# Weighted sum of expert rows: from full diagonal products to quarter products on two slots at a time

## What is computed

```
u = expert_down[idx]
act = jax.nn.gelu(jnp.einsum('thkd,td->thk', u, xb).astype(f32), approximate=False)
return jnp.einsum('thk,thkd->td', (g * act).astype(xb.dtype), expert_up[idx])
```

## Time and profile before

| | us |
|---|---|
| median of 3 runs | 4379.14 |
| lowest, highest | 4378.43, 4388.24 |
| span of the profiled execution | 4384.4 |
| PE busy | 3487.9 |
| DVE busy | 2354.8 |
| ACT busy | 1050.6 |
| POOL busy | 1348.0 |

### The profile page before, as it was taken

How to read it: one execution, slowest core, us unless ns; L and a number is a source line. 1 busy time by engine, 2 the same in 40 slices (tenths; PEclk the granted TensorE clock), 3 DMA queues, 4 the chain that set the end, 5 groups by cost and what they waited for, 6 DMA issues and landing times.

```text
span 4384.4 us, 39661 instructions
## 1 busy us (share of the span) xinstructions
PE 3487.9 (80%) x11633; PEld 1922.7 (44%) x11633; DVE 2354.8 (54%) x4730; ACT 1050.6 (24%) x3019; POOL 1348.0 (31%) x1232
## 2 busy tenths in 40 slices
PE   7699996469997687786787788778769778877876
PEld 1698774135555342352353344335325324324432
DVE  0651111746663767457546646646755755664574
ACT  1110112123341222222222222222222222222222
POOL 0020110400000343344444443434444444443442
PEclk9799997689998898898899889889889889988988
DMA  7232210642323899999999999999999999999996
GB/s 273 69 103 110 82 61 31 246 165 86 101 72 134 345 374 374 381 384 366 361 389 368 376 375 379 366 370 380 382 384 378 381 374 383 377 375 375 395 382 272
DMA packets 210634, 1269.30 MB, mean 290 GB/s; under 512 B 25875, under 2 KB 51099, under 8 KB 74060
## 3 DMA queue, kind: packets, MB, share of 16 engines
q0 software_dynamic: 159504, 1114.68, 64.3%
q1 hardware_dynamic: 50902, 152.03, 9.9%
HBM read 1218.26 MB, written 48.36 MB: 289 GB/s over the span
## 4 chain that ended last, share of the span: by engine, by line
DMA 26%; PE 25%; issue 8%; ACT 4%; POOL 3%; DVE 3%; POOLq 0%; ACTq 0%; DVEq 0%; SPq 0%
DMA e_buf<-in_experts,e_idx 26%; PE ps L1771 22%; PE ps L1502 3%; POOL e_buf L1738 3%; DVE e_buf L1840 2%; ACT e_wts L1812 2%; ACT e_diag L1816 1%; ACT e_acts L1810 1%; DMA e_buf<-in_experts,e_idxT 0%; DMA r_wq<-in_w_query 0%; POOLq L58 0%; DVE r_work L1590 0%; DVE r_row L1591 0%; DVE r_work L1587 0%; DVE r_pos L1550 0%
## 5 line engine op out<-in xcount | busy, mean ns | idle before, releaser
L1771 PE MATMUL ps<-e_buf,e_diag 128*128 128x512 f32 x4096 | 2026.0, 652 | 638.7 <-ACT e_diag L1816 635.2
L1840 DVE SCALAR_TENSOR_TENSOR e_buf<-e_buf,e_h 128x1024 f32<-128x1024 f32 x1024 | 1248.2, 1227 | 1091.6 <-DMA e_buf<-in_experts,e_idx 1075.2
L1738 POOL DMA_INDIRECT e_buf<-in_experts,e_idx x1024 | 1195.4, 1167 | 1605.1 <-PE ps L1771 1406.3
L1771 PEld LDWEIGHTS ps<-e_buf,e_diag 128*128 128x128 f32 x4096 | 836.0, 210 | 1758.4 <-issue 990.9
L1810 ACT ACTIVATE e_acts<-e_dots 128x4 f32<-128x4 f32 x256 | 52.6, 205 | 2085.0 <-DVE e_buf L1840 2076.4
L1816 ACT ACTIVATE e_diag<-ident,e_wts 128x128 f32<-128x128 f32 x1024 | 327.3, 390 | 27.8 <-ACT e_wts L1812 2.7
L1502 PEld LDWEIGHTS ps<-r_h2T,r_wq 128*128 128x128 f32 x2304 | 269.3, 193 | 34.0 <-issue 34.0
L1502 PE MATMUL ps<-r_h2T,r_wq 128*128 128x128 f32 x2304 | 269.9, 276 | 3.1 <-DMA r_wq<-in_w_query 3.1
L830 PE MATMUL ps<-xo_w_out,xo_catT 128*128 128x512 f32 x512 | 224.5, 592 | 1.7 <-DVE xo_x L863 1.7
L1812 ACT ACTIVATE e_wts<-e_acts,e_gate 128x1 f32<-128x1 f32 x1024 | 218.5, 284 | 9.2 <-ACT e_acts L1810 1.1
L74 PE MATMUL ps<-p_wth,hT_high 128*128 128x512 f32 (+1 forms) x432 | 170.6, 395 | 10.9 <-PEq L413 10.9
(11 more groups left out here) (338 smaller groups left out, 3007.2 us busy)
## 6 DMA issues: line engine op xcount, KB each, us to landing
w_mod_sb<-in_w_mod SPq DMA_DIRECT2D x12, 2048.0 KB, 8.4
e_buf<-in_experts,e_idx POOLq DMA_INDIRECT x1024, 9.1
p_wt<-in_w_rows SPq DMA_DIRECT2D x6, 2048.0 KB
proj_d<-p_ev POOLq DMA_DIRECT2D x48, 256.0 KB, 2.3
x_zgv<-proj_d SPq DMA_DIRECT2D x8, 1536.0 KB
p_w<-in_w_chan SPq DMA_DIRECT2D x20, 512.0 KB, 4.3
r_wq<-in_w_query SPq DMA_DIRECT2D x4, 2048.0 KB, 20.2
xbc_d<-p_res POOLq DMA_DIRECT2D x12, 516.0 KB, 3.0
```

Source lines behind the costliest of these rows:

```text
L1738: return pool.indirect_dma_start(out=buf[s][:], out_offset=None, in_=io["experts"], in_offset=bass.IndirectOffsetOnAxis(ap=numbers, axis=0 ...
L1771: last = nc.tensor.matmul(g.bank(cols), diag[:, k % RING, :], buf[k % RING][:, D + cols * 512:D + (cols + 1) * 512], start=(k == 0), stop= ...
L1840: V.scalar_tensor_tensor(out=down, in0=down, scalar=1.0, in1=row, op0=ALU.mult, op1=ALU.mult, accum_out=out).then_inc(sem, 1)
```

## The change

PE now takes two slots together, an even and an odd one. Each diagonal matrix is kept as its two 64x64 diagonal blocks side by side on the partitions (`diag` is 128 x 64 per slot, written from `eye2`, which has an identity in each half). A slot's sum over its upper 64 partitions and its lower 64 are separate products of 64x64 by 64x512. The even slot's products go to the partitions where their rows are, in banks 0 and 1; the odd slot's go to the other half of the partitions, in banks 2 and 3. So the four combinations of input half and output half, the quarters of the PE array, all occur. A pair has eight such products where two slots had four; PE waits for both diagonals and then releases both buffers with one increment of 2.

At the end of a tile the odd sums stand on the wrong halves. ACT copies banks 2 and 3 to `odd` (`keep_odd`), PE multiplies them with a swap matrix into banks 0 and 1 (`fold`), and DVE's `Finish.add` waits for that (`folded`) instead of `summed`. DVE builds `eye2` and `swap` once. The router's transposes move to banks 4 and 5 and wait for the scores before (`s_kept`).

PE, the first tile, before: a group of four slots, then a piece of routing. 128x512 is a product's output; each row is the program's, one per `matmul`.

```diff
--- before.py
+++ after.py
@@ -1479,8 +1479,10 @@
 
         g, nc = self.g, self.g.nc
         pe.wait_ge(self.h2_in, n * 16 + 16)
+        if not (isinstance(n, int) and n == 0):
+            pe.wait_ge(self.s_kept, n * 4)
         for k in range(KD):
-            last = nc.tensor.transpose(g.ps[:, 2 * 512 + k * P:2 * 512 + (k + 1) * P], self.h2[:, k * P:(k + 1) * P],
+            last = nc.tensor.transpose(g.ps[:, 4 * 512 + k * P:4 * 512 + (k + 1) * P], self.h2[:, k * P:(k + 1) * P],
                                        g.ident[:])
         last.then_inc(self.h2T_ps, 1)
         yield
@@ -1515,7 +1517,7 @@
 
         g, A = self.g, self.g.nc.scalar.activation
         act.wait_ge(self.h2T_ps, n + 1)
-        A(self.h2T[:].rearrange("p k r -> p (k r)"), g.ps[:, 2 * 512:4 * 512], ACT.Copy).then_inc(self.h2T_kept, 1)
+        A(self.h2T[:].rearrange("p k r -> p (k r)"), g.ps[:, 4 * 512:6 * 512], ACT.Copy).then_inc(self.h2T_kept, 1)
         yield
 
         def scores(b):
@@ -1682,7 +1684,9 @@
         buf = [sb(f"buf{s}", [P, 2 * D]) for s in range(RING)]
         idx, gate, h2 = sb("idx", [P, SLOTS], U32), sb("gate", [P, SLOTS]), sb("h2", [P, D])
         dots, acts, wts = sb("dots", [P, SLOTS]), sb("acts", [P, SLOTS]), sb("wts", [P, SLOTS])
-        diag = sb("diag", [P, RING, P])
+        diag = sb("diag", [P, RING, HALF])
+        eye2, swap, odd = sb("eye2", [P, HALF]), sb("swap", [P, P]), sb("odd", [P, D])
+        folds_ready, odd_kept, folded = sem("folds_ready"), sem("odd_kept"), sem("folded")
         h2_kept, idx_kept, generated = sem("h2_kept"), sem("idx_kept"), sem("generated")
         landed = [sem(f"landed{s}") for s in range(RING)]
         dotted, wch, weighed, summed = sem("dotted"), sem("wch"), sem("weighed"), sem("summed")
@@ -1761,26 +1765,42 @@
         def _(pe):
             pe.sem_inc(summed, RING)
             drive(rt.tensor(pe, 0), 99)
+
+            def fold(n):
+                pe.wait_ge(folds_ready, 3)
+                pe.wait_ge(odd_kept, n)
+                for cols in range(2):
+                    last = nc.tensor.matmul(g.bank(cols), swap[:], odd[:, cols * 512:(cols + 1) * 512],
+                                            start=False, stop=True)
+                last.then_inc(folded, 1)
+
             def tile(n, first):
                 route = rt.tensor(pe, n + 1)
-                for k in range(SLOTS):
+                for k in range(0, SLOTS, 2):
                     if k == 0 and not first:
+                        fold(n)
                         pe.wait_ge(fin.sum_read, n)
-                    pe.wait_ge(weighed, n * SLOTS + k + 1)
-                    for cols in range(2):
-                        last = nc.tensor.matmul(g.bank(cols), diag[:, k % RING, :],
-                                                buf[k % RING][:, D + cols * 512:D + (cols + 1) * 512],
-                                                start=(k == 0), stop=(k == SLOTS - 1))
-                    last.then_inc(summed, 1)
-                    if k % GROUP == GROUP - 1:
+                    wait_apart(pe, weighed, n * SLOTS + k + 2)
+                    for turn in range(2):
+                        for even in range(2):
+                            for r in range(2):
+                                s, cols, home = (k + even) % RING, (turn + r) % 2, (r + even) % 2
+                                part = slice(r * HALF, (r + 1) * HALF)
+                                out = g.ps[home * HALF:(home + 1) * HALF, (2 * even + cols) * 512:(2 * even + cols + 1) * 512]
+                                last = nc.tensor.matmul(out, diag[part, s, :],
+                                                        buf[s][part, D + cols * 512:D + (cols + 1) * 512],
+                                                        start=(k == 0), stop=(k == SLOTS - 2 and even == 1))
+                    last.then_inc(summed, 2)
+                    if k % GROUP == GROUP - 2:
                         drive(route, PE_PIECES.get(k // GROUP, 0))
 
             tile(0, True)
             with pe.Fori(1, NT) as n:
                 tile(n, False)
             pe.wait_ge(rt.gated, 2 * (NT + 1))
+            fold(NT)
             for m, src in enumerate((rt.num, rt.gate)):
-                last = nc.tensor.transpose(g.bank(2, cols=NS, at=m * NS), src[0:NS, :], g.ident[0:NS, 0:NS])
+                last = nc.tensor.transpose(g.bank(4, cols=NS, at=m * NS), src[0:NS, :], g.ident[0:NS, 0:NS])
             last.then_inc(turn_ps, 1)
             pe.wait_ge(fin.sum_read, NT)
             for b in range(NS):
@@ -1796,9 +1816,18 @@
             A = nc.scalar.activation
             own = rt.scalar(act, 0)
             drive(own, 10)
+
+            def keep_odd(n):
+                act.wait_ge(summed, n * SLOTS + RING)
+                A(odd[:], g.ps[:, 2 * 512:4 * 512], ACT.Copy).then_inc(odd_kept, 1)
+
             def tile(n, first):
+                if first:
+                    act.wait_ge(folds_ready, 3)
                 ch = Chain(act, wch, n * (2 + 2 * NG))
                 route = rt.scalar(act, n + 1)
+                if not first:
+                    keep_odd(n)
                 for q in range(NG):
                     if q in (0, NG // 2):
                         half = 0 if q == 0 else 1
@@ -1813,7 +1842,7 @@
                     ch.step(last)
                     for k in range(q * GROUP, (q + 1) * GROUP):
                         act.wait_ge(summed, n * SLOTS + k + 1)
-                        A(diag[:, k % RING, :], g.ident[:], ACT.Copy, scale=wts[:, k:k + 1]).then_inc(weighed, 1)
+                        A(diag[:, k % RING, :], eye2[:], ACT.Copy, scale=wts[:, k:k + 1]).then_inc(weighed, 1)
                     if first:
                         drive(own, FIRST_ACT_PIECES.get(q, 0))
                     drive(route, ACT_PIECES.get(q, 0))
@@ -1823,8 +1852,9 @@
             tile(0, True)
             with act.Fori(1, NT) as n:
                 tile(n, False)
+            keep_odd(NT)
             act.wait_ge(turn_ps, 1)
-            A(turned[:].rearrange("p a b -> p (a b)"), g.bank(2, cols=2 * NS), ACT.Copy).then_inc(turn_kept, 1)
+            A(turned[:].rearrange("p a b -> p (a b)"), g.bank(4, cols=2 * NS), ACT.Copy).then_inc(turn_kept, 1)
             fin.scalar(act, NT - 1, P)
             for b in range(NS):
                 act.wait_ge(s_dotted, b + 1)
@@ -1840,6 +1870,9 @@
                 V.scalar_tensor_tensor(out=down, in0=down, scalar=1.0, in1=row, op0=ALU.mult, op1=ALU.mult,
                                        accum_out=out).then_inc(sem, 1)
 
+            V.tensor_tensor(eye2[:], g.ident[:, 0:HALF], g.ident[:, HALF:P], ALU.add).then_inc(folds_ready, 1)
+            V.tensor_copy(swap[:, 0:HALF], g.ident[:, HALF:P]).then_inc(folds_ready, 1)
+            V.tensor_copy(swap[:, HALF:P], g.ident[:, 0:HALF]).then_inc(folds_ready, 1)
             own = rt.vector(dve, 0)
             drive(own, 23)
             dve.wait_ge(fin.consts_in, 32)
@@ -1858,7 +1891,7 @@
                         drive(route, DVE_PIECES.get(k // GROUP, 0))
                     if k == GROUP - 1 and not first:
 
-                        dve.wait_ge(summed, n * SLOTS + RING)
+                        dve.wait_ge(folded, n)
                         fin.add(dve, n - 1, P)
                     if k == 2 * GROUP - 1 and not first:
                         fin.scale(dve, n - 1, P)
@@ -1868,7 +1901,7 @@
                 tile(n, False)
             dve.wait_ge(turn_kept, 1)
             V.tensor_copy(idxT[:], turned[:, 0, :]).then_inc(idxT_ready, 1)
-            dve.wait_ge(summed, NT * SLOTS + RING)
+            dve.wait_ge(folded, NT)
             fin.add(dve, NT - 1, P)
             fin.scale(dve, NT - 1, P)
             dve.wait_ge(spread_in, 16 * NS)
```

## The result

The changed kernel takes 4440.24 us (median of 4 runs, 4434.94 to 4449.07), the kernel before 4383.69 us in the same comparison (4378.43 to 4388.74). The ratio is 1.013, with a 95% interval of 1.0111 to 1.0149: the change makes the kernel 57 us slower. The forecast was 4714 us. The sign was right; the size was not, since 335 us had been forecast for what turned out to be 57.

What follows compares the result with a forecast made beforehand. The prediction took the buffer ring as the bound: +2.48 us a turn over 128 turns, +317 us, plus 14 and 4, on 4384.4 gave 4719.4 us profiled, forecast 4714 us; range 4330 to 4980 us.

Steps and rivals of the forecast that it cites:

- The ring: Expert stage: gather, dots, weight, product, freed buffer, next gather; one turn takes 22.59 us for eight slots and decides the time.
- a + b: Measured path: fourth dot's start to first product (a), then to the first gather into the group's buffers (b).
- The first pass of B, behind it in order, can start only together with A's second.: PE's quarter products: at most two passes at once, so a pair's eight products take 9 pass times, 3.87 us at full clock.
- the rival without overlap: Quarter products on PE: 16 passes one after another for a pair, PE becomes the bound, +896 us, 5275 us; chance 0.10.
- First release +2.88 us: Path to the first freed buffers: second diagonal plus nine pass times, five slow, 6.32 us instead of 3.44.
- The second diagonal: Before a pair's products: PE waits one ACT step more, costed at 0.30 us.
- The -0.4 us from the second gather: Later releases: a pair frees two buffers at once, so the three dots behind the first take 7.32 us, not 7.73.
- Change of tile +14 us, ends +4 us: ACT's copy and PE's swap products delay PE 1.8 to 2 us, seven times; stage ends also pay for small constants.
- PE is not the bound: PE's group with routing takes 10.9 us, below the new half turn of 12.5 us.
- Four quarters at once, clock low: Rival: a pair takes 4 pass times, PE starts every group at half clock; 4370 to 4500 us, say 4400; chance 0.22.
- Four at once, clock full: Rival: four quarters overlap at full clock, -233 us of which DMA share leaves at most 144, about 4240 us; chance 0.10.
- DMA share 0.85: Expert stage: the DMA engines' busy share was to fall from 0.95 to about 0.85.

Runs made afterwards that it cites:

- the full products went in pairs: Kernel before, full products kept, but PE waits for two diagonals and releases two slots at once: 4595.1 us, ratio 1.0489.
- the experiment with filler: Changed kernel plus extra full products behind each group into unused bank 7, results never read, so PE idles less: 4362.4 us, ratio 0.9954.
- one slot at a time with filler: Changed kernel with quarter products serving and releasing one slot at a time, plus extra unread products keeping PE busy: 4186.1 us, ratio 0.9560.
- three orders tried: Changed kernel's order of a pair's products, 4440.2 us; both turns of the even slot first, 4442.1 us; all upper-half rows first, 4441.6 us.

## Why the prediction was wrong, step by step

- **What bounds the kernel.** Right. The ring from fourth dot to first free buffer decides; the experiments moved a + b from 5.18 to 8.80 us and the turn went with it from 20.94 to 24.10.
- **Passes of a quarter last as long as before; two for each product.** Right: 0.43 and 0.86 us from step to step.
- **"The first pass of B, behind it in order, can start only together with A's second."** This step failed. Rows of before show starts in order, but every product there takes the whole array; that they would stay in order with quarters was argued, not shown. Four run at once, even when the program's order is adverse. The pair takes 4 pass times, not 9. This also rules out the rival without overlap.
- **First release +2.88 us.** Measured +0.80 (a +0.11, b +0.69). With 4 slow passes for the pair my own working for the rival had +0.30, counted against a slow group; but only 79 of the 240 groups before were slow. The difference lies in the groups that had started at full clock and now start at half. The second diagonal was put at 0.30 us; a grew by 0.11, and by 0.31 where the full products went in pairs. Four diagonals now take 1.06 us instead of 1.28 (ACT's timelines), which may be a part of that.
- **The -0.4 us from the second gather.** Measured 0.42 (0.80 less 0.38). POOL's second issue comes 1.25 us behind the first in the rows shown, and 1.56 in the mean of the 240 groups, before 2.00.
- **Change of tile +14 us, ends +4 us.** The seven changes cost nothing that the trace shows; the end costs 3.2 us.
- **PE is not the bound.** Right, with more room than forecast.
- **Switching between quarter and full products, taken as 0.** Behind the last four quarter passes of a group a full pass starts 0.52 us after the last of them; a full pass behind a full one starts after 0.43 (medians over the groups with filler or routing behind them). So a switch costs about 0.1 us, and it falls behind the group's products, where the ring doesn't wait.
- **The rivals.** "Four quarters at once, clock low" is what happened: 4370 to 4500 us, said as 4400, measured 4440. The 2.0 us by which the fast half is later were set against a slack of 2.0 us taken from one turn; a mean turn 0.38 us longer says that not all of it was covered, but the slack itself was not measured. The rival got 0.22 where the forecast got 0.52. "Four at once, clock full" happened in the experiment with filler. There the price was wrong: 4240 had been worked out and 4362 came. The working took every turn of before as one that starts at half clock, while two groups in three did not, and for those a pair at full clock is no quicker than a single slot was: b was 2.87 us in them and is 2.95 in the full-clock groups with filler. Its bound of 144 us from the DMA share does not hold either: one slot at a time with filler gained 200 us.
- **DMA share 0.85.** Measured 0.94.

The range, 4330 to 4980 us, did hold 4440. It was wide because it spanned two mechanisms, and the number came from the wrong one. That "slower" came true is in part luck: the nine pass times behind it did not occur. What did make the kernel slower, the release in pairs and the low clock, stood in the sum only as terms beside them.

## What to carry to other kernels

When a resource is reused in a ring, ask what the **first** release waits for, not how long the whole batch takes: halving PE's time gained 155 us and handing back two buffers at once lost 208. An engine made faster idles more, and PE then starts at half clock more often (176 groups of 240 instead of 79); if it stands on the path there, filler work can pay, as it did by 78, 37 and 64 us. A stretch of three groups can mislead on how often that happens: count over the whole trace. A rule on order that is read off full-array products says nothing about products on parts of the array: where a sum hangs on such a step, give the other outcome as much weight.

## What the runs showed of the hardware

- Eight float32 products of 64x64 by 64x512 on four quarters run four at a time, in each of the three orders tried: 16 passes in four steps of 0.43 us (0.86 at half clock). The orders gave 4440, 4442 and 4442 us.
- In the rows shown, PE started a group at half clock after idle times of 3.08 us, 4.68 us and more, and at full clock after 0.92, 2.49 and 3.00 us. Over all traces of this case, no group with more than 5.02 us of idle right before it started at full clock; below that both occur, at half clock from 1.69 us on.
- The DMA share is no bound by itself: at 0.95, 0.99 and 1.00 the core's DMA moved 376, 398 and 407 GB/s with the same kind of gathers.
- A switch between quarter and full products on PE costs about 0.1 us: 0.52 us from start to start across it, 0.43 without.
